# The residual copied into PSUM banks before the up products of a product-key expert layer, and the last RMSNorm taken from the banks

## What is computed

```python
def peer_ffn(n, w_query, sub_keys, expert_down, expert_up):
    ...                                   # idx, gate: 16 of 16384 experts for each of 8 heads
    def block(args):
        xb, ib, gb = args
        down = expert_down[ib]
        act = jax.nn.gelu(jnp.einsum('td,tkd->tk', xb, down), approximate=False)
        up = expert_up[ib]
        return jnp.einsum('tk,tkd->td', gb.astype(xb.dtype) * act, up)
...
h = h + peer_ffn(rmsnorm(h, norm_ffn_w[l]), ...)
return rmsnorm(h, final_norm_w)
```

## Time and profile before

| | |
|---|---|
| median of 3 runs | 3534.88 us (3530.73 to 3535.65) |
| profiled execution, its own time | 3526.34 us |
| its span | 3524.6 us |
| mean granted clock of TensorE | 0.997 of full |
| PE busy / DVE busy / ACT busy | 3442.4 / 2254.7 / 1717.8 us |
| PE in 2800 to 3500 us | waits once, 2.29 us |

### The profile page before, as it was taken

One profiled execution on the slowest core, in us unless ns is written; L12 is line 12 of the kernel. 1 busy time (PEld: TensorE's weight loads), 2 busy tenths in 40 slices (PEclk: granted clock), 3 DMA queues, 4 the chain that ended last, 5 costly groups with the idle time before them and its releaser, 6 DMA issues.

```text
span 3524.6 us, 69345 instructions
## 1 busy us (share of the span) xinstructions
PE 3442.4 (98%) x23037; PEld 3164.8 (90%) x23037; DVE 2254.7 (64%) x2944; ACT 1717.8 (49%) x2494; POOL 26.3 (1%) x32
## 2 busy tenths in 40 slices
PE   8999999999999999999989999999999999999998
PEld 7999889998899999978879999999999988888887
DVE  4555444444547777774545998988889855554555
ACT  4444434444445455454435444447777644444444
POOL 0000000000000000000000000000000000000000
PEclk9999999999999999999999999999999999999999
DMA  6666665556666556556668576665666677667765
GB/s 179 175 176 176 187 179 157 158 157 178 193 188 189 174 168 186 172 155 194 188 190 209 158 171 177 175 175 160 158 160 159 166 195 192 193 193 219 197 192 166
DMA packets 484120, 628.63 MB, mean 178 GB/s; under 512 B 76832, under 2 KB 341504, under 8 KB 481792
## 3 DMA queue, kind: packets, MB, share of 16 engines
q1 hardware_dynamic: 483648, 626.51, 65.0%
q10 hardware_dynamic: 320, 0.08, 0.0%
HBM read 622.03 MB, written 4.26 MB: 178 GB/s over the span
## 4 chain that ended last, share of the span: by engine, by line
PE 81%; DVE 7%; DMA 4%; issue 3%; ACT 3%; SPq 2%; DVEq 0%; ACTq 0%
PE bank L81 26%; PE bank L82 25%; PE bank L83 25%; DMA w_raw<-in_peer_down 2%; DVE f_lo L128 2%; PE bank L1766 2%; PE bank L2176 2%; DVE w_lo L1617 1%; DVE c_xc L1200 1%; DMA f_raw<-in_w_in 1%; ACT f_hi L123 1%; SPq L458 1%; SPq L552 1%; DMA f_raw<-in_w_out 0%; SPq L465 0%
## 5 line engine op out<-in xcount | busy, mean ns | idle before, releaser
L128 DVE TENSOR_TENSOR f_lo<-f_raw,f_hi 128x768 fp32r<-128x768 f32 (+2 forms) x640 | 748.5, 1173 | 716.8 <-ACT f_hi L123 716.2
L123 ACT ACTIVATE f_hi<-f_raw 128x768 fp32r<-128x768 f32 (+2 forms) x640 | 646.2, 1016 | 752.1 <-DMA f_raw<-in_w_in 505.7
L81 PE MATMUL bank<-xT_hi,f_hi 128*128 128x256 f32 x2560 | 738.7, 289 | 26.9 <-DVE f_lo L128 12.0
L82 PE MATMUL bank<-xT_lo,f_hi 128*128 128x256 f32 x2560 | 723.9, 283 | 0.0
L83 PE MATMUL bank<-xT_hi,f_lo 128*128 128x256 f32 x2560 | 723.9, 283 | 0.0
L81 PE MATMUL bank<-xT_hi,w_hi 128*128 128x256 f32 x2048 | 587.4, 287 | 9.8 <-DVE w_lo L1617 9.6
L82 PE MATMUL bank<-xT_lo,w_hi 128*128 128x256 f32 x2048 | 579.1, 283 | 0.0
L83 PE MATMUL bank<-xT_hi,w_lo 128*128 128x256 f32 x2048 | 579.1, 283 | 0.0
L1704 DVE TENSOR_TENSOR w_lo<-w_raw,w_hi 128x1024 fp32r<-128x1024 f32 x256 | 313.7, 1225 | 340.1 <-PE bank L83 333.1
L81 PEld LDWEIGHTS bank<-xT_hi,f_hi 128*128 128x128 f32 x2560 | 490.2, 191 | 42.1 <-DVE f_lo L128 15.6
L82 PEld LDWEIGHTS bank<-xT_lo,f_hi 128*128 128x128 f32 x2560 | 490.5, 192 | 1.9 <-issue 1.7
(11 more groups left out here) (274 smaller groups left out, 4833.4 us busy)
## 6 DMA issues: line engine op xcount, KB each, us to landing
w_raw<-in_peer_down SPq DMA_DIRECT2D x1024, 128.0 KB, 3.4
w_raw<-in_peer_up SPq DMA_DIRECT2D x1024, 128.0 KB, 2.6
f_raw<-in_w_in SPq DMA_DIRECT2D x1024, 96.0 KB, 2.4
f_raw<-in_w_in SPq DMA_DIRECT2D x256, 256.0 KB, 2.9
f_raw<-in_w_in SPq DMA_DIRECT2D x384, 128.0 KB, 2.8
f_raw<-in_w_branch_c SPq DMA_DIRECT2D x256, 128.0 KB, 2.8
f_raw<-in_w_branch_a SPq DMA_DIRECT2D x128, 128.0 KB, 2.8
f_raw<-in_w_branch_b SPq DMA_DIRECT2D x128, 128.0 KB, 2.8
```

What stands on the lines that cost most here:

```text
L81: nc.tensor.matmul(out, lhs[0], rhs[0], start=start, stop=False, skip_group_check=True)
L82: nc.tensor.matmul(out, lhs[0], rhs[1], start=False, stop=False, skip_group_check=True)
L123: nc.scalar.activation(self.hi[u % 4][:, 0:cols], self.raw[u % 4][:, 0:cols], ACT.Copy).then_inc(self.hi_done, 1)
L128: nc.vector.tensor_tensor(self.lo[u % 4][:, 0:cols], self.raw[u % 4][:, 0:cols], self.hi[u % 4][:, 0:cols].bitcast(F32), ALU.subtract).the ...
```

## The change

- The residual's eight blocks of 128x512 are numbered `4 * tb + n`. Six of them (`H_ORDER`) are loaded one bank at a time into three small tiles `h_part` and copied by ACT into their accumulator banks (`seed`), so that the up products add to them. The block to bank table is now `U_BANK`.
- Ahead of that PE writes each of the six banks once with a matmul whose result the seed overwrites, at `j` = 124, and signals `m_mm` 65.
- SP's program has the last four down units and first four up units written out, with the six loads (`h_load`, 256 KB each) in between and a wait for three seeds (`z_seed`).
- Blocks 0 and 1 keep the addition by DVE at the end; only they are loaded late (one load of 512 KB in place of two of 1 MB).
- The up stage's first unit takes token block 1 first; the second waits for all six seeds. The last two units go by tokens: u254 and u255 for token block 0, then both for token block 1.
- Squares and scalings read the banks in pieces of 512 columns; token block 0 is finished before token block 1.

The diff, with the renamed tiles and semaphores left out:

```diff
-        z_h = place("z_h", [P, TB, D], 0)
+        h_part = [place("z_h0", [P, 512], at_chosen), place("z_h1", [P, 512], at_second),
+                  nc.alloc_sbuf_tensor_at("z_h2", [P, 512], F32, offset=low)]
+        H_ORDER = (4, 5, 2, 3, 6, 7)
+        U_BANK = (6, 7, 2, 3, 4, 5, 0, 1)
+        z_h = place("z_h", [P, 1024], 0)
...
-                with sp.Fori(0, EU // NR) as it:
+                def h_load(n):
+                    b = H_ORDER[n]
+                    sp.dma_start(h_part[n % 3][:, :], h_dram[b // 4 * P:b // 4 * P + P, b % 4 * 512:b % 4 * 512 + 512]
+                                 ).then_inc(z_in, 16)
+                with sp.Fori(0, EU // NR - 1) as it:
                     e_load(it)
-                with sp.Fori(0, 40) as it:
+                sp.wait_ge(m_mm, T // 4)
+                sp.wait_ge(m_first, T // 4)
+                for n in range(3):
+                    h_load(n)
+                e_load(EU // NR - 1, range(2))
+                sp.wait_ge(z_seed, 3)
+                for n in range(3, 6):
+                    h_load(n)
+                e_load(EU // NR - 1, range(2, 4))
+                u_load(0)
+                with sp.Fori(1, 40) as it:
                     u_load(it)
                 sp.wait_ge(u_lo, 60)
-                for tb in range(TB):
-                    sp.dma_start(z_h[:, tb, :], h_dram[tb * P:(tb + 1) * P, :]).then_inc(z_in, 16)
+                sp.dma_start(z_h[:, :], h_dram[0:P, 0:1024]).then_inc(z_in, 16)
...
+                def seed(n0, n1):
+                    act.wait_ge(z_in, 16 * n1)
+                    for n in range(n0, n1):
+                        nc.scalar.activation(bank[U_BANK[H_ORDER[n]]][:, :], h_part[n % 3][:, :], ACT.Copy).then_inc(z_seed, 1)
...
+                    if j == PN - 2:
+                        act.wait_ge(m_mm, T // 4 + 1)
+                        seed(0, 3)
...
                 coef_hi(0, 0)
                 gelu(PN - 1)
                 u_split(0, 1)
+                seed(3, 6)
                 act.wait_ge(weighed, PN - SPLIT)
                 coef_hi(1, 1)
...
                 def z_square(tb, half):
-                    act.wait_ge(z_added, 4 * half + 2 * tb + 2)
                     if tb or half:
-                        act.wait_ge(z_sq, 2 * half + tb)
-                    nc.scalar.activation(z_junk[:, :], z_h[:, tb, half * 1024:half * 1024 + 1024], ACT.Square,
-                                         accum_out=z_ssq[:, tb, half:half + 1]).then_inc(z_sq, 1)
+                        act.wait_ge(z_sq, 4 * tb + 2 * half)
+                    if tb or half:
+                        act.wait_ge(z_done, 2 * tb + half + 1)
+                    for cc in range(2):
+                        if tb == half == 0:
+                            act.wait_ge(z_total, cc + 1)
+                        if cc:
+                            act.wait_ge(z_sq, 4 * tb + 2 * half + 1)
+                        nc.scalar.activation(z_junk[:, :], total_of(tb, 2 * half + cc), ACT.Square,
+                                             accum_out=z_ssq[:, tb, 2 * half + cc:2 * half + cc + 1]).then_inc(z_sq, 1)
...
                 z_square(0, 0)
-                z_square(1, 0)
                 z_square(0, 1)
                 z_sqrt(0)
+                z_square(1, 0)
                 z_square(1, 1)
                 z_sqrt(1)
...
                 def z_scale(tb):
+                    dve.wait_ge(z_sq, 4 * tb + 4)
+                    v.tensor_reduce(z_sum[:, tb:tb + 1], z_ssq[:, tb, :], AX.X, ALU.add).then_inc(z_total, 1)
                     dve.wait_ge(z_root, tb + 1)
                     v.reciprocal(z_rstd[:, tb:tb + 1], z_std[:, tb:tb + 1]).then_inc(z_total, 1)
-                    dve.wait_ge(z_total, 2 * tb + 2)
-                    for half in range(2):
-                        at = slice(half * 1024, half * 1024 + 1024)
-                        v.scalar_tensor_tensor(out=result[:, tb, at], in0=z_h[:, tb, at], scalar=z_rstd[:, tb:tb + 1],
+                    dve.wait_ge(z_total, 2 * tb + 4)
+                    for n in range(4):
+                        at = slice(n * 512, n * 512 + 512)
+                        v.scalar_tensor_tensor(out=result[:, tb, at], in0=total_of(tb, n),
+                                               scalar=z_rstd[:, tb:tb + 1],
                                                in1=wide[:, at], op0=ALU.mult, op1=ALU.mult).then_inc(z_norm, 1)
...
+                dve.wait_ge(z_in, 128)
+                dve.wait_ge(z_done, 1)
+                for n in range(2):
+                    v.tensor_tensor(total_of(0, n), total_of(0, n), bank[U_BANK[n]][:, :], ALU.add).then_inc(z_total, 1)
                 z_scale(0)
-                z_pair(1)
                 z_scale(1)
...
+                    if j == PN - 4:
+                        pe.wait_ge(m_mult, T // 4)
+                        for b in (4, 5, 2, 3, 0, 1):
+                            last = nc.tensor.matmul(bank[b][:, :], xT_hi[:, 0, 0:P], xT_hi[:, 0:2, :],
+                                                    start=True, stop=True, skip_group_check=True)
+                        last.then_inc(m_mm, 1)
                     products(0, 2 * j + 1, j)
...
+                def u_half(u, tb, first=False):
+                    cf = (cf_hi[u // 2 % 2], cf_lo[u // 2 % 2])
+                    t = slice(tb * P, (tb + 1) * P)
+                    for cc in range(2):
+                        at = slice(cc * 512, (cc + 1) * 512)
+                        last = tri_matmul(bank[U_BANK[4 * tb + 2 * (u % 2) + cc]][:, :], (cf[0][:, t], cf[1][:, t]),
+                                          (hi[u % 3][:, at], lo[u % 2][:, at]), start=first, stop=True)
+                    return last
+
+                def u_ready(it, u):
                     if u % 2 == 0:
                         pe.wait_ge(u_lo, 6 * it + u // 2 + 1)
                     pe.wait_ge(lo_done, 12 * it + U0 + u + 1)
-                    cf = (cf_hi[u // 2 % 2], cf_lo[u // 2 % 2])
...
+                def u_products(it, u):
+                    u_ready(it, u)
+                    u_half(u, 0)
+                    u_half(u, 1).then_inc(used, 1)
+                u_ready(0, 0)
+                pe.wait_ge(z_seed, 2)
+                u_half(0, 1)
+                pe.wait_ge(weighed, PN - SPLIT)
+                u_half(0, 0, True).then_inc(used, 1)
+                u_ready(0, 1)
+                pe.wait_ge(z_seed, 6)
+                u_half(1, 0)
+                u_half(1, 1).then_inc(used, 1)
+                for u in range(2, 12):
+                    u_products(0, u)
...
+                for u in range(2):
+                    u_products(21, u)
+                u_ready(21, 2)
+                u_half(2, 0).then_inc(z_done, 1)
+                u_ready(21, 3)
+                u_half(3, 0).then_inc(z_done, 1)
+                u_half(2, 1).then_inc(z_done, 1)
+                u_half(3, 1).then_inc(z_done, 1)
```

More of the change, by code:

```diff
@@ L411, in program @@
         z_in = sem("z_in")
-        z_half = sem("z_half")
-        z_added = sem("z_added")
+        z_done = sem("z_done")
+        z_seed = sem("z_seeded")
         z_sq = sem("z_squared")
@@ L545, in q_load, with e_load @@
                                      q_rows[32 * a:32 * a + 32, 2 * u:2 * u + 2, ds(it * 512, 512)]).then_inc(raw_full[u % NR], 16)
-                def e_load(it):
-                    for u in range(NR):
+                def e_load(it, units=range(NR)):
+                    for u in units:
                         sp.wait_ge(lo_done, E0 + NR * it + u - 3)
@@ L553, in e_load, with u_load @@
                                          e_rows[:, :, ds(2 * it + u // 2, 1), at:at + 256]).then_inc(raw_full[u], 16)
-                def u_load(it):
-                    for u in range(NR):
+                def u_load(it, units=range(NR)):
+                    for u in units:
                         sp.wait_ge(lo_done, U0 + NR * it + u - 3)
@@ L583, in _ @@
                         at = slice(half * 1024, half * 1024 + 1024)
-                        sp.wait_ge(z_norm, 2 * tb + half + 1)
+                        sp.wait_ge(z_norm, 4 * tb + 2 * half + 2)
                         sp.dma_start(out[0, tb * P:(tb + 1) * P, at], result[:, tb, at]).then_inc(z_out, 16)
@@ L1055, in _ @@
                 u_body(21, 4, False)
+                total_of = lambda tb, n: z_h[:, n * 512:n * 512 + 512] if 4 * tb + n < 2 else bank[U_BANK[4 * tb + n]][:, :]
                 def z_square(tb, half):
-                    act.wait_ge(z_added, 4 * half + 2 * tb + 2)
                     if tb or half:
-                        act.wait_ge(z_sq, 2 * half + tb)
-                    nc.scalar.activation(z_junk[:, :], z_h[:, tb, half * 1024:half * 1024 + 1024], ACT.Square,
-                                         accum_out=z_ssq[:, tb, half:half + 1]).then_inc(z_sq, 1)
+                        act.wait_ge(z_sq, 4 * tb + 2 * half)
[8 more added lines that the diff above has]
```

(25 more changed lines are left out.)

14 lines of the change are left out of this document (2 added, 12 removed).

## The result

| | before | changed |
|---|---|---|
| median of 12 runs, us | 3534.45 (3527.82 to 3538.78) | 3541.36 (3535.55 to 3548.02) |
| ratio to before | 1 | 1.0028 (95% interval 1.0020 to 1.0035) |
| profiled execution, span | 3524.6 | 3538.1 |

A forecast was written before the change was run, and what follows sets the result against it. PE was taken to bound the kernel, busy for 98% of the span. Terms 11.9 + 3.1 + 0.5 - 2.4 - 1.7 = +11.4 us on 3534.88 gave 3546.3 us, range 3539.5 to 3551.5.

The forecast's parts named there:

- six matmuls: Bank-preparing matmuls of 512 columns on PE, ahead of the up products: +1.4 us.
- first three residual loads: On SP ahead of d252's load: 0 us, as d252 had 2.7 us of room; 1 at most.
- SP's wait, beyond the matmuls: At d253: d254's loads queue behind SP's wait for three seeds; PE stands still 10.5 us (+11.9 with the matmuls' 1.4).
- slow clock: Behind PE's long wait at d253: clock at half speed for a while, +3.1 us, bounds 1.6 and 3.4.
- seeds four to six: ACT makes them between u1's split and u2's coefficients, delaying PE: +0.5 us, bounds 0.2 and 1.2.
- late loads: Near 3236 us, 1.5 MB instead of 3 MB removes PE's 2.29 us wait: -2.4 us, bounds -2.4 and -1.
- the end: After the last up units: additions start sooner and squares go in smaller pieces, -1.7 us, bounds -1 and -2.2.
- rival 4: Up stage: the late wait stays, half the load being enough to stop PE; adds up to 2.4 us, 3548.7; chance 0.07.
- Rivals 1 and 3: After d252: clock stays up, 3543.2 us (0.14 with early landing); or d254's load covered, PE never stops, 3532.7 us (0.10).
- rival 2: The first three residual loads hold d252 too: 5 us late would add 2.3 us, 3548.6; chance 0.09.
- early landing: d254's load landing 2.9 us sooner by the skill's DMA fit: sum 8.5 in place of 11.4 us.

The follow-up runs named there:

- Experiment 2: Changed kernel, SP's loads reordered: those of d254, d255, u0 go ahead of the seed wait and last three residual loads; 3519.26 us against 3533.14, ratio to before 0.9981.
- experiment 4: Changed kernel with 32 unread filler matmuls of 512 columns on PE between d252 and d253; ratio to before 1.0012; with 42, one run only.
- experiment 3: Kernel before, with SP waiting for PE's end of d251 ahead of d254's and d255's loads, no residual loads or seeds; ratio to before 1.0017.

## Why the prediction was right, term by term

| term | forecast, us | measured, us | where |
|---|---|---|---|
| six matmuls | +1.4 | +1.4 | 2795.54 to the next start, 2796.93 |
| first three residual loads | 0 (up to 1) | +0.4 | d251 started 0.4 us late, waiting 0.24 |
| SP's wait, beyond the matmuls | +10.5 | +10.5 | d252 to d253, 13.4 us for 2.88 |
| slow clock | +3.1 (1.6 to 3.4) | +2.1 | d253 to u0, 10.77 for 8.64 |
| seeds four to six | +0.5 | +0.3 | u0 to u1, 3.20 for 2.94 |
| late loads | -2.4 (-2.4 to -1) | -1.3 | 0.96 for 2.29 |
| the end | -1.7 | -2.1 | u254's start to last scaling, 12.17 for 14.29 |
| sum | +11.4 | +11.3 | by places 746.14 - 734.90 = 11.2 |

- **SP's wait** was the step that decided, and held in each of its parts: third seed done at 2808.17, SP on at 2808.20 where 0.2 us were allowed, the loads 0.47 us apart where 0.5 were (these are written out, without address arithmetic between them), landing 6.0 for 5.2. The errors mostly cancel: PE started d253 at 2819.36 - 2.33 = 2817.0 for a forecast 2816.6. Experiment 2 shows that the place of d254's loads behind the wait does it, and experiment 3 that a wait alone makes 5.87 us of it.
- **The clock** fell, as after the 8.82 us wait of the earlier trace rows, but came back 4.6 us after PE did (5.4 in the second profile), where it had taken about 6.2 there. The term was taken from a single instance; it was too large by 1 us, and within its bounds.
- **First residual loads**: the 2.7 us of room were nearly right, and all used. d252 came at 2800.68 - 2.33 = 2798.35, 3.1 us later than before.
- **Late loads**: rival 4 happened in part in this profile. Over the kernels with 1.5 MB there the wait was 0, 0, 0.27, 0.27, 0.96 and 1.17 us, with 3 MB 2.29, 2.50 and 3.68. Fewer bytes are less wait, but a fixed value was too sharp a claim. Behind the 2.50 and the 3.68 us the clock fell as well, which the forecast, with the 2.29 us wait alone before it, did not reckon with.
- **The end** was 0.4 us better than forecast. The hold of PE for u255's low part was there (u255 began 0.19 us late) and, as said, cost nothing.
- Rivals 1 and 3 are refuted by the clock's rows and by the 10.27 us; rival 2 happened to the extent of 0.4 us. The early landing that the Trainium skill's fit for the GpSimd path (DMA: Bandwidth & Descriptors, Anatomy of one DMA) would give did not come: 2.3 us by an estimate from it, 5.97 us here, on SP's path.
- The median came out 4.9 us under the forecast, while the places of this pair of profiles agree to 0.2 us (over both pairs they give +10.0). The two medians are each uncertain by some us, and the ratio's interval goes up to 12 us. But the second timing of the changed kernel has an interval of 3 to 9.5 us, which ends below the forecast, so the size was probably forecast some us too high.
- That the table's sum comes to 11.3 for 11.4 is in part luck: its terms are off by +0.4, -1.0, -0.2, +1.1 and -0.4 us, and these cancel.
- The forecast took 0.2% for what can be told from no change; the intervals of these ratios are half as wide, about 0.1% either way.

## What to carry to other kernels

A wait put into the program that also issues the critical loads costs what stands behind it, not what it guards. Here it cost 10.3 us of PE, for three residual loads that ACT first read some 22 us after their issue, and moving the loads of three units ahead of it in SP's program took that long wait away. Count for each load how much room it has against its consumer (d254 had 0.7 us, d252 2.7), and put new transfers and their waits in front of the one with the most. What the bytes do is then small: the kernels with the residual in the banks and the wait moved came out 0.1 to 0.2% faster than before. The late loads apart alone gave 0.14 to 0.15%.

## What was not expected of the hardware

- The clock can fall after the idleness is over. In experiment 4 PE was idle for 3.33 us and the fall came when it was busy again. The same is seen in an earlier part of the reordered kernel's profile, behind a wait of 4.12 us that left the first matmul at full speed:

```profile
1825.47 0.50 PE L81 MATMUL bank<-f_hi,xT_hi 128*128 128x512 f32 x1 [4.12 <-DVE f_lo L128]
...
1824.00:1826.00 2.00, 0.53 (x2) 0.48 (x3) 1.23 (x1) 1.97 (x6) 0.00 (x0) 1.00 1.05 242
1826.00:1828.00 2.00, 2.00 (x6) 1.56 (x6) 1.23 (x1) 1.12 (x2) 0.00 (x0) 0.52 0.75 176
1830.00:1832.00 2.00, 2.00 (x17) 1.87 (x16) 0.00 (x0) 0.57 (x2) 0.00 (x0) 1.00 0.40 117
```

- The length of PE's wait does not settle by itself whether the clock falls. A wait of 2.29 us left it at 1.00 in the first profile of the kernel before, and so did waits of 0.75 to 1.17 us elsewhere. In its second profile, in the same place, a wait of 2.50 us had it at 0.50 behind it:

```profile
3255.22 0.79 PE L81 MATMUL bank<-w_hi,u_coef_hi 128*128 128x512 f32 x1 [2.50 <-DVE w_lo L1704]
...
3256.00:3258.00 2.00, 2.00 (x7) 1.52 (x6) 1.56 (x2) 1.08 (x3) 0.00 (x0) 0.50 1.08 240
```

- The runs' spread is made far from the change, in code that is the same in all thirteen profiles. In the stage of the output projection PE waits once for long, for loads of `w_out` behind 2 MB of `x`: for 4.10 to 8.82 us, and the slow clock comes with it. Between there and 2780 us PE waits 13 to 25 times for low parts of down units, for 8.8 to 16.9 us in all. The last scattered product started anywhere from 2779.89 to 2799.80 us. That is why changes of 2 us are told by places here, and not by medians.
